# Pooling by shifted sums behind a transposed first projection, in a two-layer model block

## What is computed

```python
def multiscale_pool(u):
    ...
    cs = jnp.cumsum(uf, axis=1)
    for g, w in enumerate((2, 4, 8, 16)):
        c = cs[..., g * 192:(g + 1) * 192]
        prev = jnp.pad(c, ((0, 0), (w, 0), (0, 0)))[:, :s]
        cnt = jnp.minimum(pos + 1, w)
        outs.append((c - prev) / cnt)
    return jnp.concatenate(outs, axis=-1) - uf

def pool_layer(...):
    proj = rmsnorm(x, norm_mix) @ w_in
    u_pool, q_mem = proj[..., :768], proj[..., 768:]
    pooled = multiscale_pool(u_pool).reshape(b, s, 4, 192)
    grouped = jnp.einsum("bsgc,gcd->bsgd", pooled, w_group).reshape(b, s, 768) * scale
    mk, mv = memory_kv(mem, mem_norm, w_mem_kv)
    mem_out = memory_attention(q_mem, mk, mv)
    x = x + jnp.concatenate([grouped, mem_out], axis=-1) @ w_out
    return x + swiglu(rmsnorm(x, norm_ffn), w_gu, w_down)
```

## Time and profile before

| | |
|---|---|
| median of 3 runs | 954.86 us (954.58 to 955.42) |
| the profiled execution, its own time | 954.67 us |
| its span | 953.0 us |
| TensorE busy | 944.5 us, 99% |
| VectorE busy | 622.1 us, 65% |
| ScalarE busy | 514.6 us, 54% |
| GpSimd busy | 30.7 us, 3% |
| chain that ended last: TensorE | 98% |

### The profile page before, as it was taken

One profiled execution on the slowest core, in us unless ns is written; L12 is line 12 of the kernel. 1 busy time (PEld: TensorE's weight loads), 2 busy tenths in 40 slices (PEclk: granted clock), 3 DMA queues, 4 the chain that ended last, 5 costly groups with the idle time before them and its releaser, 6 DMA issues.

```text
span 953.0 us, 13086 instructions
## 1 busy us (share of the span) xinstructions
PE 944.5 (99%) x5102; PEld 784.9 (82%) x5102; DVE 622.1 (65%) x858; ACT 514.6 (54%) x687; POOL 30.7 (3%) x71
## 2 busy tenths in 40 slices
PE   9999999999999999999999999999999999999997
PEld 6878888888888887888888888877777888888886
DVE  6554877776457366577777447688884776775444
ACT  6754555554346575655555336667685455544333
POOL 0400000000000000000000001000310000000000
PEclk9999999999999999999999999999999999999999
DMA  9715555555555420655555657643224555555561
GB/s 363 234 50 187 189 181 197 196 176 184 215 177 178 175 89 1 221 177 183 202 188 176 220 199 302 220 145 134 89 99 167 177 177 180 189 200 203 188 209 44
DMA packets 25723, 168.66 MB, mean 177 GB/s; under 512 B 2749, under 2 KB 3627, under 8 KB 6475
## 3 DMA queue, kind: packets, MB, share of 16 engines
q1 hardware_dynamic: 24320, 163.39, 48.6%
q0 software_dynamic: 1264, 4.57, 1.2%
q10 hardware_dynamic: 91, 0.04, 0.0%
HBM read 166.91 MB, written 1.08 MB: 176 GB/s over the span
## 4 chain that ended last, share of the span: by engine, by line
PE 98%; DVE 1%; DMA 1%; ACT 0%; issue 0%; SPq 0%; DVEq 0%; ACTq 0%
PE ps L1592 49%; PE ps L1916 23%; PE ps L1919 12%; PE ps L1709 1%; PE ps L2303 1%; PE ps L2313 1%; PE ps L2332 1%; PE ps L1831 1%; PE ps L2038 1%; PE ps L1822 1%; PE ps L1668 1%; DMA raw<-in_in 1%; PE ps L1794 1%; PE ps L1871 0%; PE ps L1841 0%; PE ps L2151 0%
## 5 line engine op out<-in xcount | busy, mean ns | idle before, releaser
L966 DVE TENSOR_TENSOR w_both<-raw,w_both 128x2048 fp32r<-128x2048 f32 x149 | 339.6, 2287 | 157.4 <-ACT w_both L489 157.4
L489 ACT ACTIVATE w_both<-raw 128x2048 fp32r<-128x2048 f32 x149 | 283.4, 1912 | 134.4 <-DMA raw<-in_down 40.9
L1916 PE MATMUL ps<-a_both,w_both 128*128 128x512 f32 x960 | 264.3, 395 | 0.0
L1592 PE MATMUL ps<-w_both,a_both 128*128 128x512 f32 (+1 forms) x816 | 191.0, 388 | 0.0
L1916 PEld LDWEIGHTS ps<-a_both,w_both 128*128 128x128 f32 x960 | 163.3, 189 | 21.2
L1592 PEld LDWEIGHTS ps<-w_both,a_both 128*128 128x128 f32 x816 | 146.8, 188 | 31.1 <-issue 2.6
L1919 PEld LDWEIGHTS ps<-a_both,w_both 128*128 128x128 f32 x960 | 149.0, 189 | 21.5
L1592 PE MATMUL ps<-w_both,h_hi 128*128 128x512 f32 x576 | 154.5, 389 | 0.0
L1919 PE MATMUL ps<-a_both,w_both 128*128 128x256 f32 x960 | 154.5, 281 | 0.0
L1592 PEld LDWEIGHTS ps<-w_both,h_hi 128*128 128x128 f32 x576 | 107.8, 188 | 22.2
L1592 PE MATMUL ps<-w_both,h_lo 128*128 128x512 f32 x288 | 88.7, 389 | 0.0
(11 more groups left out here) (271 smaller groups left out, 762.3 us busy)
## 6 DMA issues: line engine op xcount, KB each, us to landing
raw<-in_a_gu SPq DMA_DIRECT2D x22, 1024.0 KB, 4.7
raw<-in_b_gu SPq DMA_DIRECT2D x22, 1024.0 KB, 4.7
raw<-in_up SPq DMA_DIRECT2D x16, 1024.0 KB, 4.8
raw<-in_down SPq DMA_DIRECT2D x16, 1024.0 KB, 4.8
raw<-in_a_down SPq DMA_DIRECT2D x11, 1024.0 KB, 4.7
raw<-in_b_down SPq DMA_DIRECT2D x11, 1024.0 KB, 4.7
raw<-in_front SPq DMA_DIRECT2D x8, 1024.0 KB, 4.8
raw<-in_gates SPq DMA_DIRECT2D x8, 1024.0 KB, 4.8
```

The lines of the kernel that those rows point to most:

```text
L489: A_(ring(w_hi, us)[:, 0:n], ring(raw, us)[:, 0:n], ACT.Copy).then_inc(s_hi, 1)
L966: V.tensor_tensor(ring(w_lo, us)[:, 0:n], ring(raw, us)[:, 0:n], ring(w_hi, us)[:, 0:n].bitcast(fp32), ALU.subtract).then_inc(s_lo, 1)
L1592: ins = MM(ps[:, b + T, 0:wd], chT(parts[ap_], c, T), wp[wp_][:, off:off + wd], start=(c == first and pn == 0), stop=(c == last and pn == 2))
L1916: MM(bank(4 * k + s).rearrange("p (z n) -> p z n", z=2), ring(w_hi, us)[:, cols[s]], both_parts[:, :, c, :], start=c == 0, stop=False)
```

## The change

`in` is now made with weights as the stationary operand, 128 output channels at a time, and 256 positions moving (`in_slices`): channels lie on partitions at once. The inverse root of each position is turned into a row by two transposes and copied to all partitions (`root_rows`). VectorE multiplies the result with it into `win_u`, six chunks of 128 channels, each with 16 blank columns ahead, and straight into the queries `qTA`. On `win_u` VectorE adds shifted copies: sums over 2, from them over 4, 8 and 16, each only on the chunks that need it (`window_sum`); it repairs the first 16 positions with factors in `early` and makes sum / w minus itself in eight instructions. ScalarE rounds the result to `pool_hi`, GpSimd makes `pool_lo`. GpSimd has also written the group weights as hi and lo into blocks of 128 x 128 with blanks (`g_hi`, `g_lo`). Each `grouped` then is 6 or 9 products of 256 columns in the fast format over full tiles. The pooling products, `poolM` and its load, and the transposes of the queries are gone. The lists of all engines between `mem_a` and `a_out` are written in a new order.

```diff
+PAD = 16
+WINDOWS = (2, 4, 8, 16)
+N_BLANK = 4 + sum(w - 1 for w in WINDOWS)
...
-            sp.dma_start(poolM[:, :], A["pool"]).then_inc(s_pin, 16)
             job("mem_a", 0, 1)
-            sp.dma_start(wgrp[0:96, :].rearrange("p (c n) -> p c n", c=8),
-                         A["a_w_group"].rearrange("g (c p) n -> p (g c) n", p=96)).then_inc(s_pin, 16)
+            sp.dma_start(wgrp[:, :].rearrange("p (c n) -> p c n", c=6),
+                         A["a_w_group"].rearrange("g r n -> (g r) n").rearrange("(c p) n -> p c n", p=P)).then_inc(s_pin, 16)
...
+            blank(windows(win_u)[:, :, 0:PAD])
+            blank(g_hi[:, :].bitcast(fp32))
+            blank(g_lo[:, :].bitcast(fp32))
+            blank(early[:, :], 1.0)
+            pool.wait_ge(s_blank, blanks[0])
+            for g, w in enumerate(WINDOWS):
+                for t in range(w - 1):
+                    blank(early[:, PAD * g + t:PAD * g + t + 1], float(w) / (t + 1))
+            assert blanks[0] == N_BLANK
+            pool.wait_ge(s_pin, 16)
+            for n, (rows, part, at) in enumerate(GROUP_PARTS):
+                dst, src = (t[rows, :].rearrange("p (z n) -> p z n", z=2)[:, :, lo:lo + 192]
+                            for t, lo in ((g_hi, at), (wgrp, 192 * part)))
+                if n:
+                    pool.wait_ge(s_gw, 2 * n)
+                nc.gpsimd.tensor_copy(dst, src).then_inc(s_gw, 1)
+                pool.wait_ge(s_gw, 2 * n + 1)
+                nc.gpsimd.tensor_tensor(g_lo[rows, :].rearrange("p (z n) -> p z n", z=2)[:, :, at:at + 192], src,
+                                        dst.bitcast(fp32), ALU.subtract).then_inc(s_gw, 1)
+            for n in range(2):
+                pool.wait_ge(s_poolh, n + 1)
+                v = slice(3 * S * n, 3 * S * n + 3 * S)
+                nc.gpsimd.tensor_tensor(pool_lo[:, v].rearrange("p (c n) -> p c n", n=S),
+                                        windows(win_u)[:, 3 * n:3 * n + 3, PAD:],
+                                        pool_hi[:, v].rearrange("p (c n) -> p c n", n=S).bitcast(fp32),
+                                        ALU.subtract).then_inc(s_pooll, 1)
...
+            act.wait_ge(s_rT0, 1)
+            A_(root_rows[:, :], bank(4, 0, S), ACT.Copy).then_inc(s_rb0, 1)
...
-            for r in range(4):
-                act.wait_ge(s_pool, r + 1)
-                A_(poolT[0:96, 512 * r:512 * r + 512], ps[0:96, 4 + r, :], ACT.Copy).then_inc(s_poolc, 1)
...
-            q_copy(0, qTA[:, :], 4, HD ** -0.5)
             q_copy(1, mkTA[:, :], 5, 1.0)
-            split_hi(U0["a_out"])
+            for n in range(2):
+                act.wait_ge(s_pool, 4 * n + 4)
+                A_(pool_hi[:, 3 * S * n:3 * S * n + 3 * S].rearrange("p (c n) -> p c n", n=S),
+                   windows(win_u)[:, 3 * n:3 * n + 3, PAD:], ACT.Copy).then_inc(s_poolh, 1)
             grouped_hi(0)
-            split_hi(U0["a_out"] + 1)
-            grouped_hi(1)
             mem_exps("mem_a", 0)
             mem_exps("mem_a", 1)
+            grouped_hi(1)
+            mem_exps("mem_a", 2)
+            mem_exps("mem_a", 3)
+            split_hi(U0["a_out"])
             grouped_hi(2)
-            mem_exps("mem_a", 2)
+            mem_copy("mem_a", 0)
             grouped_hi(3)
-            mem_exps("mem_a", 3)
-            mem_copy("mem_a", 0)
+            split_hi(U0["a_out"] + 1)
+            mem_hi("mem_a", 0)
             grouped_hi(4)
             mem_copy("mem_a", 1)
             grouped_hi(5)
-            mem_hi("mem_a", 0)
...
+            dve.wait_ge(s_half, HALF["in"] + 1)
+            dve.wait_ge(s_rb0, 1)
+            V.tensor_tensor(U[:, 0:4, PAD:], pair_banks(PAIR[G0["in"]]).rearrange("p b (z n) -> p (b z) n", z=2),
+                            rows_over(4), ALU.mult).then_inc(s_gdve, 1)
             split_lo(U0["mem_a"])
             transposed_lo(k_m, to_m, (3,))
+            dve.wait_ge(s_mm, U0["in"] + 4)
+            right = 2 * PAIR[G0["in"] + 1]
+            V.tensor_tensor(U[:, 4:6, PAD:], bank(right).rearrange("p (z n) -> p z n", z=2), rows_over(2), ALU.mult)
+            V.scalar_tensor_tensor(qTA[:, :].rearrange("p (z n) -> p z n", z=2),
+                                   bank(right + 1).rearrange("p (z n) -> p z n", z=2), HD ** -0.5, rows_over(2),
+                                   ALU.mult, ALU.mult).then_inc(s_gdve, 1)
             split_lo(U0["mem_a"] + 1)
+            dve.wait_ge(s_gdve, emptied(G0["in"] + 1, "dve"))
+            dve.wait_ge(s_blank, N_BLANK)
+
+            def window_sum(dst, src, c0, w):
+                link(V.tensor_tensor(dst[:, c0:, w - 1:], src[:, c0:, w - 1:], src[:, c0:, w // 2 - 1:S + PAD - w // 2],
+                                     ALU.add))
+            window_sum(SA, U, 0, 2)
             inverse_rms("mem").then_inc(s_rst, 1)
-            presplit("mem_b")
-            presplit("a_out")
+            split_lo(U0["mem_b"])
+            window_sum(SB_, SA, 1, 4)
+            window_sum(SA, SB_, 3, 8)
+            window_sum(SB_, SA, 4, 16)
+            ends = early[:, :].rearrange("p (g n) -> p g n", n=PAD)
+            for sums, rows, c0, g in ((SA, slice(0, P), 0, 0), (SA, slice(0, 64), 1, 0),
+                                      (SB_, slice(64, P), 1, 1), (SB_, slice(0, P), 2, 1)):
+                v = sums[rows, c0:c0 + 4:3, PAD:2 * PAD]
+                marked(V.tensor_tensor(v, v, ends[rows, g:g + 3:2], ALU.mult))
+            dve.wait_ge(s_dve, chain[0])
+            for half in range(2):
+                for sums, rows, c0, g in ((SA, slice(0, P), 0, 0), (SA, slice(0, 64), 1, 0),
+                                          (SB_, slice(64, P), 1, 1), (SB_, slice(0, P), 2, 1)):
+                    c = c0 + 3 * half
+                    V.scalar_tensor_tensor(U[rows, c, PAD:], sums[rows, c, PAD:], 1.0 / WINDOWS[g + 2 * half],
+                                           U[rows, c, PAD:], ALU.mult, ALU.subtract).then_inc(s_pool, 1)
+            split_lo(U0["mem_b"] + 1)
 
             def grouped_lo(c):
 
...
                 g = 8 * len(GAMMAS) + c
                 V.scalar_tensor_tensor(ch(a_lo, c), bank(c % 2, 0, S), gam[:, g:g + 1], ch(a_hi, c).bitcast(fp32),
                                        ALU.mult, ALU.subtract).then_inc(s_glo, 1)
-            grouped_lo(0)
-            grouped_lo(1)
             mem_max("mem_a", 0)
             mem_max("mem_a", 1)
+            grouped_lo(0)
+            mem_norm("mem_a", 0)
+            mem_norm("mem_a", 1)
+            grouped_lo(1)
             mem_max("mem_a", 2)
-            mem_norm("mem_a", 0)
             mem_max("mem_a", 3)
-            mem_norm("mem_a", 1)
             grouped_lo(2)
+            split_lo(U0["a_out"])
+            mem_copy("mem_a", 0)
+            grouped_lo(3)
             mem_norm("mem_a", 2)
-            grouped_lo(3)
             mem_norm("mem_a", 3)
-            mem_copy("mem_a", 0)
+            split_lo(U0["a_out"] + 1)
+            mem_lo("mem_a", 0)
             grouped_lo(4)
             mem_copy("mem_a", 1)
             grouped_lo(5)
-            mem_lo("mem_a", 0)
             mem_lo("mem_a", 1)
...
+            def in_slices(us, c, nb, parts, which, start=False, stop=False):
+
+                for s in range(4):
+                    b = 2 * PAIR[G0["in"] + nb] + s // 2
+                    at = D * (c % 2) + 512 * nb + P * s
+                    ins = MM(bank(b, S * (s % 2), S * (s % 2) + S), ring(parts, us)[:, at:at + P], ch(which, c),
+                             start=start and s % 2 == 0, stop=stop, skip_group_check=True)
+                return ins
+
             def in_piece(j, nb, k):
 
-                return mult_pieces(U0["in"] + j, [(2 * j + k, 2 * PAIR[G0["in"] + nb], 512, D * k + 512 * nb)], AH, 0, KC - 1,
-                                   need=in_need)
+                us, c = U0["in"] + j, 2 * j + k
+                in_need(c)
+                in_slices(us, c, nb, w_hi, a_hi)
+                in_slices(us, c, nb, w_lo, a_hi)
+                return in_slices(us, c, nb, w_hi, a_lo, stop=c == KC - 1)
...
+            pe.wait_ge(s_rst, NORM["a_mix"] + 1)
+            pe.wait_ge(s_nlo, 4 * SET["mem"] + 1)
+            for T in range(2):
+                ins = nc.tensor.transpose(bank(4, P * T, P * T + P), rst["a_mix"][:, T:T + 1].broadcast_to([P, P]), ident[:, :])
+            ins.then_inc(s_rT0, 1)
...
-            pe.wait_ge(s_pin, 32)
-            pe.wait_ge(s_gact, emptied(G0["in"] + 1, "act"))
-            for r in range(4):
-                for c in (2 * r, 2 * r + 1):
-                    o = S * (c % 2)
-                    for n, (T, lo, hi) in enumerate(POOLED):
-                        m0 = 1024 * T + S * (c // 2)
-                        ins = MM(ps[0:96, 4 + r, o + lo:o + hi], tok(projA, D, T)[:, 96 * c:96 * c + 96],
-                                 poolM[:, m0 + lo:m0 + hi], start=(n == 0), stop=(n == 2), skip_group_check=True)
-                ins.then_inc(s_pool, 1)
...
```

(41 more changed lines are left out.)

67 lines of the change are left out of this document (36 added, 31 removed).

## The result

The changed kernel takes 957.38 us, median of 14 runs (956.43 to 958.38); the kernel before, run beside it on the same chip, 955.11 (954.58 to 955.43, 14 runs). The ratio is 1.0025, 95% interval 1.0018 to 1.0033: slower by 2.3 us, just over the 1.9 us that can be told from no change. The forecast was 954.8 us, no change that can be told. The profiled execution took 957.96, its span 956.2, so 3.2 us more than the span before. That is one of the longer executions of the changed kernel against one of the shorter ones of the kernel before: the profiled pair shows 3.3 us of difference in time where the medians show 2.3.

The account below looks back on a forecast made before the run. TensorE, busy 944.5 of 953.0 us, was taken to bound the kernel. Its work fell 5.5 us, but a 5.0 us wait for VectorE and smaller terms gave that back: 954.67 + 0.1 = 954.8 us, range 952.2 to 958.3.

Parts of the forecast that it names:

- case A: TensorE's wait before the output projection gives back the saved work, clock kept: 954.8 us, chance 0.40.
- case B: The same TensorE wait also drops the clock, products behind it at half pace: +1.3, 956.1 us, chance 0.25.
- The wait: TensorE, from 60.8 us, waits 5.0 us for VectorE's copy of the transposed probabilities, released at 65.9.
- Under 3.4 it is wrong: Sign near 61 us: TensorE waits about 5 us for the copy to pb; under 3.4 refutes the main claim.
- GpSimd's hold: GpSimd's first 768-column pass blocks VectorE between the seventh and eighth subtraction for 1.8 us.
- The cause of the wait: Before the copies: splits of the first output unit (1.83 ScalarE, 2.2 VectorE), plus GpSimd holding VectorE 1.8 us.
- rival C: Between the subtractions GpSimd holds VectorE 3.0 us instead of 1.8: +2.3, with the clock 958.3 us, chance 0.18.
- The price of the clock: Behind TensorE's gap: 3.4 us at half pace, 1.7 lost, some 0.4 hidden in waits: +1.3 us.
- The first projection: 192 products of 256 columns at 0.1175 instead of 96 of 512 at 0.2275: +0.7 us, 0.2 hidden.
- TensorE's own work: Before the output projection: pooling products and four transposes gone, projection dearer, root transposes added, grouped products cheaper: -5.5 us.
- GpSimd's weights: Group weights land 2 or 3 us sooner; GpSimd's eight passes end near 31, costing VectorE's split up to 1.0 us.
- Behind 90 us: Later stages: everything unchanged in length; a TensorE wait there would be unforeseen.

Follow-up runs that it names:

- the filled one: Changed kernel with 34 thrown-away products of 256 columns put into TensorE's 4.6 us gap before the values product: 955.67 us.
- the narrow products alone: Kernel before with its first projection in 192 products of 256 columns instead of 96 of 512: 955.76 us against 954.89.
- the reordered kernel: Changed kernel with copies of transposed probabilities, second normalisations and grouped remainder 3 ahead of the first output unit's split, second unit's split behind grouped remainder 5: 951.54 us.

## Why the prediction was wrong

The mechanism on the engines was right; the step that failed is the choice between case A (clock kept) and case B (clock lost), and one term of the sum was too small. In the profiled pair the forecast's own chain adds up: the copy was released at 67.05 instead of 65.9 (1.15), what stands behind it takes 6.6 at full clock instead of 6.4 (0.2), and the lost clock adds 1.9. Together that is the way from the forecast 72.3 to the measured 75.52. Point by point:

- **The wait.** Forecast 5.0 us, copy released at 65.9; measured 4.6, released at 67.05. Of those 1.15 us the late start is at most 0.6; the other half arose on VectorE between the window sums and the eighth subtraction:

```profile
47.26 0.29 DVE L1195 TENSOR_TENSOR win_a<-win_a,early 128x32 f32<-128x32 f32 x2
...
48.03 0.75 DVE L1201 SCALAR_TENSOR_TENSOR win_u<-win_a,win_u 128x256 f32<-128x256 f32 x2
...
49.61 0.75 DVE L1201 SCALAR_TENSOR_TENSOR win_u<-win_a,win_u 128x256 f32<-128x256 f32 x2
```

  The edge factors took 0.77 where 0.5 was forecast, the first four subtractions 1.58 where 1.3 was (0.39 each, not 0.34). From the end of the eighth subtraction to the end of the copy it is 14.1 us, as forecast. "Under 3.4 it is wrong": it isn't. (The prediction's gap without GpSimd's hold, 3.4, is 3.2 by its own numbers, 5.0 - 1.8.)
- **The cause of the wait.** Forecast: the first output unit's splits in front of both copies, and GpSimd's hold of 1.8. Shown by the kernels that take each away: without the splits ahead of the copies the wait is 0.6, without the hold 4.3. The pass took 1.86 and held VectorE for 1.5; rival C's 3.0, from the mean row of 0.998, did not come.
- **The clock: the step that failed.** I had the end of the kernel as the one instance, 3.7 us without work before the fall, and a gap of 5.0, and still gave "kept" 0.40 and "lost" 0.25. The argument against B was that one instance makes no bound. But it was evidence on the wrong side of 5.0: it showed a fall after a shorter gap, and nothing in the trace showed a gap survived. By that row B should have been the likeliest case. The runs showed that 4.6 us lose the clock (mean under 0.998 in twelve of fourteen executions), and that even 2.5 can. The rule cited there, that a gap throttles TensorE and the products behind start cold, agrees with the traces at 4.6 us (1.97 instead of 1.08 for the first eight products). The DMA waits in its example (the Trainium skill, TensorE: Matmul & The Clock Gate, HAM oscillation) are 3 to 5 us; here 2.5 were enough in the profiled execution, and there the first eight products still ran at full pace.
- **The price of the clock.** Forecast 1.3, from 3.4 us at half pace less 0.4 that waits hide; measured 1.7 (changed kernel less the filled one; 1.5 to 1.9 by the way of counting, above) and 1.85 in the kernel before. Nothing of it was hidden: everything behind the gap was late already. B with that price is 954.8 + 1.7 = 956.5, and the measured median is 0.9 above that; 0.25 of it is the kernel before, which stood at 955.11 beside the changed kernel and not at 954.86. The rest is smaller than the late release of the profiled pair, 1.15. How much of it belongs to which term in the median execution stays open, since the changed kernel has one trace.
- **The first projection.** Forecast 0.1175 a product, +0.5 net, and +0.2 for the transposes of the roots; 0.120 measured, +0.7 in the trace of the narrow products alone and +0.9 in its median. In the changed kernel the whole stretch, transposes included, is 34.07 - 8.42 = 25.65, +0.8. So it was too low by 0.1 to 0.4.
- **TensorE's own work.** Forecast -5.5. From the first product to the output projection the reordered kernel takes 69.52 - 8.38 = 61.1, of which 1.3 are waits; before 72.33 - 7.83 = 64.5. So -4.7. Beside the projection, the grouped products are short of the forecast: by their rows in the reordered kernel the 42 take 5.2 us, 15 of them 1.80 in the chain of the filled one, where 4.9 was forecast and 5.5 stood before. In the changed kernel this error cost nothing: TensorE came to the gap later and waited less, and VectorE set the end.
- **GpSimd's weights.** Forecast: landed 2 or 3 us sooner than 27.7, the passes end near 31. In the timeline of the changed kernel the first pass began at 25.1 and the last, below, reached into the split:

```profile
30.80 1.01 POOL L452 TENSOR_TENSOR g_lo<-wgrp,g_hi 128x384 fp32r<-128x384 f32 x1
30.84 3.12 DVE L1007 TENSOR_TENSOR w_both<-raw,w_both 128x2048 fp32r<-128x2048 f32 x1
```

  The split took 3.12 instead of 2.3. TensorE's memory stage began at 34.07, 0.7 after the 33.4 forecast, with a start up to 0.6 late, and TensorE did not wait there: no loss.
- **Behind 90 us** nothing was forecast and nothing came.

The time fell in the range, 952.2 to 958.3, which had been drawn out for B and C; "slower" had 0.33. The range held by that width and not by case A.

## What to carry to other kernels

When a change takes work from the engine that bounds a kernel, walk the other engines' orders through the same stretch: the work removed was worth nothing until the items that TensorE waits for stood ahead of those it needs 6 to 7 us later. And price a wait of TensorE at more than its length: if the trace shows the granted clock falling after a gap shorter than yours, count the half-speed stretch behind it as the likely case and not as a risk. A test for it is cheap: fill the gap with products whose result is thrown away, and see if the kernel gets faster. And look at the spread of a kernel's executions before taking one trace for all of them: where the mean granted clock differs between executions, one profile shows only one of the cases.

## What was not expected of the hardware

- A wait of 2.5 us brought TensorE from 2.4 to 1.2 GHz in the profiled execution and, by the mean granted clock, in six of nine; 3.2 us in eight of eleven; 1.4 us in none of eleven. All of them came behind a stretch from 8 us on in which TensorE had waited for 0.5 or 0.6 us.
- The clock can fall after the wait is over: with 2.5 us of waiting the first eight products behind it ran at full pace and the next step did not.
- The cost of the fall does not follow the length of the gap. By medians it is 1.5 us at 2.5 (957.17 less 955.67; by the mean, three of those nine executions kept the clock), 1.7 at 4.6, 1.85 at 6.4. In single traces, from the product behind the gap to the output projection, against 6.60 with the gap filled, it is 1.3 at 2.5 (74.86 - 66.92 = 7.94), 2.3 at 4.3 and 1.9 at 4.6.
- The pace of the warm-up varies from execution to execution, enough to move the first product between 7.52 and 8.71 us in the twelve traces.
